# Stage ends by token tiles: tile 0's sums end first, and the next stage begins with two units in natural form

## The chip, the cores and the metric

The kernel runs on one core of one Trainium2 chip. The metric is the device time of one execution in microseconds; lower is better. Times are medians of a few runs on the chip, and the profile is one further execution. The engines are called PE (TensorE, the matrix engine), DVE (VectorE), ACT (ScalarE), POOL (GpSimd) and SP (SyncE, which here only issues DMAs).

## The reference

256 tokens of width 1024, float32, pass three layers. The first two (`first_block`) each mix tokens and then apply a feed-forward stage, with a layer norm after each; the second layer's feed-forward stage is a mixture of experts. The third (`second_block`) uses RMS norms ahead of its parts.

```python
for layer in range(2):
    mix = _mixer_ab(x, ...) if layer == 0 else _mixer_cd(x, ...)
    x = _layernorm(ALPHA * x + mix, ln_g[layer, 0], ln_b[layer, 0])
    ffn = _swiglu(x, w1_dense, w3_dense, w2_dense) if layer == 0 else _moe(x, w_router, w1_moe, w3_moe, w2_moe)
    x = _layernorm(ALPHA * x + ffn, ln_g[layer, 1], ln_b[layer, 1])
h = x
u = rms_norm(h, mix_norm_g)
proj = u @ w_in                       # q, k, v and the two halves of a gated convolution
h = h + concat(attention(q, k, v), conv(glu_a, glu_g)) @ w_out
u = rms_norm(h, ffn_norm_g)
h = h + (silu(u @ w_gate) * (u @ w_up)) @ w_down
return rms_norm(h, final_norm_g)
```

`_swiglu(x, w1, w3, w2)` is `(silu(x @ w1) * (x @ w3)) @ w2`, with a hidden width of 2816. `_mixer_cd` projects x to queries, keys and values of two attentions (c and d, 8 heads each) and to 8 forget columns, whose cumulated log-sigmoids are added to the scores of the first attention. The experts have a hidden width of 3584, and each token goes to 2 of 8.

## The kernel before

**Units and halves.** All weights come in units of 1 MB (128 partitions x 2048 floats) through a ring of 6 slots, loaded by SP in the order of their use. A product in full precision takes each operand as an upper part (rounded to PE's fp32r) and a lower part (the rest), and adds three products: upper x upper, upper x lower, lower x upper (`thirds`, L611 to L614). ACT writes the upper part of each unit (`upper`, L1270), DVE the lower (`lower`, L1697), into two buffers in turn; POOL makes the lower part of the first unit after the first mixer, after the dense FFN and after the third mixer (its `lower`, L2300). The experts use three buffers. `upper` waits until the unit before the last has been used, and PE waits for both parts of a unit (`taken`).

**Token tiles.** The tokens are two tiles of 128. A unit of columns is used in one of two forms. In the transposed form the weights are stationary and the 256 tokens move (`proj_transposed`, and `up`, L841 and L843, where upper and lower tokens move together in one matmul of 512 columns). In the natural form the tokens are stationary and 256 weight columns move (`proj_natural`). A unit of rows (`out_unit` for a mixer's output, `down` for an FFN's) adds to four PSUM banks of 512 columns: two tiles x two column halves.

**A stage end.** When the last unit has been added, DVE adds the residual (L1721), ACT forms the mean and the squared deviations (`deviations`, L1372 to L1374), POOL the reciprocal root (L2291), DVE centres (L1756) and scales (L1761) each tile; PE transposes the rows (L690), ACT copies their upper part (L1276), DVE their lower part (L1707); and the next stage's first unit begins. While PE has nothing to do it runs matmuls of ones whose results nobody uses (`keep_busy`, L605; `spins` says how many).

**The order of work** is written out by hand for each engine, and the engines meet by semaphores. In a mixer, the steps of the attention stand in numbered gaps, two per unit: lists such as `CD_SCORES` give for each step (scores, transposed probabilities, values) the gap in which it stands, and `CD_OUT_TURNED` the gaps in which finished heads are transposed for the output. `cd_gap(i)` exists on PE, ACT and DVE. The forget columns come from a narrow projection (`narrow`) at the start of the second mixer, and their lower parts from DVE (L2051).

## Time and profile before

| | us |
|---|---|
| median of 3 runs | 1795.64 (1794.57 to 1800.24) |
| the profiled execution | 1797.47 |
| its span, first to last instruction | 1795.6 |
| busy: PE | 1764.1 |
| busy: DVE | 1349.8 |
| busy: ACT | 1143.2 |
| busy: POOL | 156.9 |

The mean granted clock of TensorE was 0.997 of full speed. The span is what the page and the views of the trace divide up; the execution's own time is 1.9 us more. Matmuls are pipelined: a row's duration is longer than the distance to the next row, and the distance is the cost. The fillers count as busy.

### The profile page before, as it was taken

To read this page: it belongs to the slowest core of one execution; us is meant where nothing else is said; L and a number is where in the kernel's file an instruction comes from. 1 tells how busy PE (TensorE), PEld (TensorE's weight loads), DVE (VectorE), ACT (ScalarE), POOL (GpSimd) and SP (SyncE) were. 2 spreads that over 40 slices of the span, in tenths; PEclk is the share of its full clock that TensorE was granted. 3 is DMA by queue.
4 is the path that set the end of the run, shared out by engine and by line. 5 is a ranking of instruction groups with operands and counts; after the bars stand their busy time and mean duration, and the time that the engine had idled before them with its cause. 6 is when DMAs were issued, how large, how long until landed. Compare 5 with 4: busy or idle time off the path is not lost.

```text
span 1795.6 us, 24768 instructions
## 1 busy us (share of the span) xinstructions
PE 1764.1 (98%) x9332; PEld 1480.6 (82%) x9332; DVE 1349.8 (75%) x1252; ACT 1143.2 (64%) x1160; POOL 156.9 (9%) x107
## 2 busy tenths in 40 slices
PE   9999999999999999999999999999999999899998
PEld 7897888889878888888888888888888879878886
DVE  3765655545588888888888888888888888866555
ACT  4654545545467777777777777777777774545443
POOL 0002000100041000000000000000000105510000
PEclk9999999999999999999999999999999999999999
DMA  9845555543489999999999999999999985445550
GB/s 291 263 149 172 188 187 187 176 146 124 154 279 370 394 368 393 359 381 390 352 393 375 365 394 359 379 391 350 394 377 363 396 290 187 141 132 190 189 188 30
DMA packets 260196, 502.86 MB, mean 280 GB/s; under 512 B 15068, under 2 KB 101653, under 8 KB 259758
## 3 DMA queue, kind: packets, MB, share of 16 engines
q1 hardware_dynamic: 252160, 474.67, 74.6%
q0 software_dynamic: 7072, 26.69, 4.8%
q10 hardware_dynamic: 910, 0.76, 0.1%
q8 instruction: 36, 0.59, 0.1%
q14 instruction: 18, 0.15, 0.0%
HBM read 494.18 MB, written 12.65 MB: 282 GB/s over the span
## 4 chain that ended last, share of the span: by engine, by line
PE 90%; DVE 5%; ACT 2%; POOL 2%; issue 1%; DMA 0%; DVEq 0%; POOLq 0%; SPq 0%; ACTq 0%
PE psum L611 24%; PE psum L614 23%; PE psum L613 23%; PE psum L841 9%; PE psum L843 5%; DVE psum L2215 2%; PE psum L1126 1%; ACT wh L1270 1%; PE psum L750 1%; POOL wl L2300 1%; PE psum L718 1%; DVE x L1761 1%; POOL rstd L2291 1%; DMA ring<-in_w_in_ab 0%; PE psum L734 0%
## 5 line engine op out<-in xcount | busy, mean ns | idle before, releaser
L1697 DVE TENSOR_TENSOR wl<-ring,wh 128x2048 fp32r<-128x2048 f32 x437 | 1001.4, 2292 | 252.3 <-ACT wh L1270 251.2
L1270 ACT ACTIVATE wh<-ring 128x2048 fp32r<-128x2048 f32 x450 | 862.2, 1916 | 270.9 <-PE psum L611 169.6
L611 PE MATMUL psum<-wh,xT 128*128 128x512 f32 (+1 forms) x1136 | 431.6, 380 | 1.4 <-DVE xT L1853 1.1
L614 PE MATMUL psum<-wh,xT 128*128 128x512 f32 (+1 forms) x1136 | 424.5, 374 | 0.0
L613 PE MATMUL psum<-wl,xT 128*128 128x512 f32 (+1 forms) x1136 | 424.4, 374 | 0.0
L611 PE MATMUL psum<-wh,wnh 128*128 128x512 f32 x672 | 266.3, 396 | 0.5 <-DVE wnl L1853 0.5
L614 PE MATMUL psum<-wh,wnl 128*128 128x512 f32 x672 | 263.6, 392 | 0.0
L613 PE MATMUL psum<-wl,wnh 128*128 128x512 f32 x672 | 263.5, 392 | 0.0
L611 PEld LDWEIGHTS psum<-wh,xT 128*128 128x128 f32 x1136 | 214.2, 189 | 43.5 <-issue 3.0
L841 PE MATMUL psum<-xT,wh 128*128 128x512 f32 x704 | 249.1, 398 | 0.4 <-DVE xT L1707 0.4
L614 PEld LDWEIGHTS psum<-wh,xT 128*128 128x128 f32 x1136 | 214.0, 188 | 39.9
L613 PEld LDWEIGHTS psum<-wl,xT 128*128 128x128 f32 x1136 | 214.3, 189 | 37.0
L843 PE MATMUL psum<-xT,wl 128*128 128x256 f32 x704 | 197.4, 280 | 0.0
L841 PEld LDWEIGHTS psum<-xT,wh 128*128 128x128 f32 x704 | 132.2, 188 | 33.6 <-issue 1.2
L611 PEld LDWEIGHTS psum<-wh,wnh 128*128 128x128 f32 x672 | 126.3, 188 | 28.4 <-issue 1.4
L614 PEld LDWEIGHTS psum<-wh,wnl 128*128 128x128 f32 x672 | 126.2, 188 | 28.4
L613 PEld LDWEIGHTS psum<-wl,wnh 128*128 128x128 f32 x672 | 126.3, 188 | 25.8
L843 PEld LDWEIGHTS psum<-xT,wl 128*128 128x128 f32 x704 | 132.9, 189 | 0.7
L611 PE MATMUL psum<-xT,wh 128*128 128x256 f32 x384 | 112.4, 293 | 2.0 <-DVE wl L1697 1.7
L613 PE MATMUL psum<-xT,wh 128*128 128x256 f32 x384 | 109.9, 286 | 0.0
L614 PE MATMUL psum<-xT,wl 128*128 128x256 f32 x384 | 109.9, 286 | 0.0
L611 PEld LDWEIGHTS psum<-xT,wh 128*128 128x128 f32 x384 | 74.9, 195 | 4.4 <-issue 3.3
(303 smaller groups left out, 1410.9 us busy)
## 6 DMA issues: line engine op xcount, KB each, us to landing
ring<-in_w_moe SPq DMA_DIRECT2D x336, 1024.0 KB, 6.9
ring<-in_w_dense SPq DMA_DIRECT2D x33, 1024.0 KB, 5.2
ring<-in_w_in_ab SPq DMA_DIRECT2D x14, 1024.0 KB, 11.2
ring<-in_w_in_cd SPq DMA_DIRECT2D x12, 1024.0 KB, 5.3
ring<-in_w_gate SPq DMA_DIRECT2D x11, 1024.0 KB, 5.3
ring<-in_w_up SPq DMA_DIRECT2D x11, 1024.0 KB, 5.3
ring<-in_w_down SPq DMA_DIRECT2D x11, 1024.0 KB, 4.9
ring<-in_w_in SPq DMA_DIRECT2D x6, 1024.0 KB, 8.2
```

The source lines that it names most:

```text
L611: last = pe.matmul(o, a[0], b_[0], start=first, stop=False)
L613: pe.matmul(o, a[0], b_[1], start=False, stop=False)
L614: return pe.matmul(o, a[1], b_[0], start=False, stop=final)
L718: last = pe.matmul(o, q[rows, hp, t * P:(t + 1) * P], k[rows, hp, 0:n], start=True, stop=not (forget or masked))
L750: last = pe.matmul(to[:, o:o + HD], pT[:, g % 2, (2 * hh + s) * P:(2 * hh + s + 1) * P], v[:, s, h * HD:(h + 1) * HD], start=(s == 0), sto ...
L841: first_of(pe.matmul(ps.rearrange("p (a t) -> p a t", a=2), h_[:, k, m], xT_both[:, :, k, :], start=k == 0, stop=False))
L843: last = pe.matmul(ps[:, 0:T], l_[:, k, m], xTh[:, k, :], start=False, stop=k == KT - 1)
L1126: last = pe.transpose(bank[2 + c % 2][:, f * P:(f + 1) * P], mg[:, f * P:(f + 1) * P], ident[:, :])
L1270: act.activation(upper_half[i], ring[:, u_, :], ACT.Copy).then_inc(hi_ready[s_], 1)
L1697: dve.tensor_tensor(lower_half[i], ring[:, u_, :], upper_half[i].bitcast(F32), ALU.subtract)\
L1761: dve.scalar_tensor_tensor(x[:, t, s_], src[:, t, s_], rstd[:, t:t + 1], w[:, 1, s_], ALU.mult, ALU.add).then_inc(x_ready if t else x_half, 1)
L2215: last = dve.scalar_tensor_tensor(summed(c, j), upad[:, c, j:j + T], cw[:, c, j:j + 1], summed(c, j - 1), ALU.mult, ALU.add)
```

## The change

- The last two units of each mixer and of each FFN are added in another order (`out_last`, `down_last`): all of tile 0's sums end before the last three chunks of tile 1's.
- `tile_norms` takes the place of `layer_norm` after the first mixer, the dense FFN and the second mixer. Tile 0's mean and variance come from DVE (bn_stats, bn_aggr), tile 1's from row sums and ACT's squares as before (`second_deviations`). The RMS norm ahead of the last FFN is ordered likewise.
- After the first mixer, the dense FFN and the third mixer the next stage begins with `tile_pair`: two units in natural form, accumulated in banks 4 and 5 in four pieces (tile x half of the rows). With each piece PE adds both units' upper weight halves, and transposes the next piece in between; the products with the lower weight halves follow in a pass of their own, one unit after the other. For the FFNs the pair is the first unit of w1 and of w3, whose gated product is formed in natural form and transposed (`turn_hidden`); for the second mixer it is the two units of the first attention's values.
- DVE makes the lower parts that POOL made at the stage ends.
- These stages use a third buffer of halves, and `upper` waits there for one unit less (`used_before`).
- The steps of the first attention in the second mixer stand two gaps later, the next four steps one; the forget rows' lower parts stand ahead of one unit's lower half.
- The last unit of each FFN has its hidden parts in another order (`silus_last`, `gates_last`).

The core of the diff, its indentation shortened:

```diff
-CD_SCORES = [0, 1, 2, 3, 4, 5, 6, 7, 10, 11, 12, 13, 16, 17, 18, 19]
-CD_TURNED = [2, 3, 4, 5, 6, 7, 8, 9, 12, 13, 14, 15, 17, 18, 19, 20]
-CD_VALUES = [3, 4, 5, 6, 7, 8, 9, 10, 13, 14, 15, 16, 18, 19, 20, 21]
-CD_OUT_TURNED = [8, 14, 20, 22]
+CD_SCORES = [2, 3, 4, 5, 6, 7, 8, 9, 11, 12, 13, 14, 16, 17, 18, 19]
+CD_TURNED = [4, 5, 6, 7, 8, 9, 10, 11, 13, 14, 15, 16, 17, 18, 19, 20]
+CD_VALUES = [5, 6, 7, 8, 9, 10, 11, 12, 14, 15, 16, 17, 18, 19, 20, 21]
+CD_OUT_TURNED = [10, 14, 20, 22]
...
-CD_ORDER = [CD[n + h] + 256 * i for h in "cd" for i in range(2) for n in "qkv"]
+CD_ORDER = [CD["vc"], CD["vc"] + 256] + [CD[n + "c"] + 256 * i for i in range(2) for n in "qk"] + \
+   [CD[n + "d"] + 256 * i for i in range(2) for n in "qkv"]
...
+        after_out, after_ffn = (18, 53) if self.s == 0 else (11, 11 + 3 * NCH_D)
+        if self.s == 1 and n == 0:
+            half = 2
+        elif n >= LENGTHS[0]:
+            half = (LENGTHS[0] + 2 - n) % 3
+        elif after_out <= n < after_ffn:
+            half = (n - 16) % 3 if self.s == 0 else (after_out + 2 - n) % 3
         else:
-            half = (n + 1) % 2
+            half = n % 2
...
+    def used_before(self):
+
+        n = self.n - 1
+        third = n < 54 if self.s == 0 else True
+        back = 2 if n > (18 if self.s == 0 else 11) and third or n >= LENGTHS[0] else 1
+        return n - back + self.more
...
+    def tile_pair(src, n, done):
+
+        units = []
+        for j in range(2):
+            u_, loads, i, at_ = halves.place()
+            units.append([w.rearrange("p (k n) -> p k n", k=KT) for w in (upper_half[i], lower_half[i])]
+                         + [u_, loads, at_])
+        turn_piece(src, n, 0, 0)
+        keep_busy(5, 3)
+        for i, (t, kh) in enumerate(PIECES):
+            m = slice(t * P, (t + 1) * P)
+            pe.wait_ge(tr_low, trs[0] + i + 1)
+            for j, (h_, l_, u_, loads, at_) in enumerate(units):
+                o = bank[4 + j][:, t * 256:(t + 1) * 256]
+                if i == 0:
+                    pe.wait_ge(hi_ready[halves.s], at_ + 1)
+                for k in range(4 * kh, 4 * kh + 4):
+                    pe.matmul(o, xTh[:, k, m], h_[:, k, :], start=t == 0 and k == 0, stop=False)
+                    pe.matmul(o, xTl[:, k, m], h_[:, k, :], start=False, stop=False)
+                if j == 0 and i < 3:
+                    turn_piece(src, n, *PIECES[i + 1])
+        trs[0] += 4
+        for j, (h_, l_, u_, loads, at_) in enumerate(units):
+            pe.wait_ge(taken[halves.s][u_], loads)
+            for t in range(TT):
+                m = slice(t * P, (t + 1) * P)
+                for k in range(KT):
+                    last = pe.matmul(bank[4 + j][:, t * 256:(t + 1) * 256], xTh[:, k, m], l_[:, k, :],
+                                     start=False, stop=t == 1 and k == KT - 1)
+                    first_of(last)
+            last.then_inc(done[j], 1)
+            split_done()
...
+        two = split_unit("rows")
+        pe.wait_ge(o_low, turned)
+        sums_of(2, two, 0, (0, 1))
+        if gap is not None:
+            gap()
+        sums_of(2, two, 1, (0,))
+        three = split_unit("rows")
+        pe.wait_ge(o_low, turned + 1)
+        sums_of(3, three, 0, (0, 1))
+        sums_of(2, two, 1, (1,))
+        split_done()
+        sums_of(3, three, 1, (0, 1))
+        split_done()
+        sums[0] += 1
...
+        tile_pair(src, n, (one_done[s], up_done[s]))
         pe.wait_ge(sums_evac, sums[0])
-        up(s, 0)
-        up(s, 2)
-        down(s, 0, True, False)
+        up(s, 2, middle=turn_hidden)
+        down(s, 0, True)
...
+    assert steps[0] == STEPS_PAIR
+    tile_pair(x, 2, (step_done, step_done))
+    steps[0] += 2
+    for i in range(2):
+        projected["v", CD_FIRST // 4 + i] = STEPS_PAIR + 1 + i
+    pe.wait_ge(sums_evac, sums[0])
     narrow(later, 0, 8)
...
-    transposes(x, 3, spins=(16, 5, 2))
+    for j in range(2):
+        out_unit(j, 4 + j + 1, lambda: cd_gap(18 + 2 * j))
+        cd_gap(19 + 2 * j)
+    out_last(7, lambda: cd_gap(22))
+
+
+    transposes(x, 3, spins=(5, 7, 2))
...
+    def silu_pair(s):
+
+        act.wait_ge(one_done[s], 1)
+        act.activation(mh, bank[4][:, :], ACT.Silu).then_inc(silu_done[s], 1)
+        upper()
+        upper()
+        act.wait_ge(up_done[s], 2)
+        act.activation(hTh[:, 0, :, :], bank[6].rearrange("p (f t) -> p f t", f=2), ACT.Copy).then_inc(h_high[s], 1)
...
+    upper(a_pv, 8)
     upper()
-    deviations(0, y, u)
-    upper(sums_done, 1)
-    copy_transposed()
+    copy_piece(0, 0)
+    second_deviations(0)
+    for p in PIECES[1:]:
+        copy_piece(*p)
     ffn(0)
...
+    upper()
+    upper()
+    copy_piece(0, 0)
+    second_deviations(1)
+    for p in PIECES[1:]:
+        copy_piece(*p)
+    upper()
+    copy_step(nv[:, :, 0:256])
+    upper()
+    copy_step(nv[:, :, 256:512])
...
+    of_out = [(x2_ready, i + 1) for i in range(4)]
+    squares(of_out, (0,))
     upper()
-    squares([(x2_ready, i + 1) for i in range(4)])
-    upper(sums_done, 3)
-    copy_transposed()
+    copy_piece(0, 0)
+    squares(of_out, (1,))
+    for p in PIECES[1:]:
+        copy_piece(*p)
...
+        link(residual_half(0, 0, y, ALPHA, done, count))
+        dve.bn_stats(stat[:, 12:18], y[:, 0, 0:512])
+        residual_half(0, 1, y, ALPHA, done, count).then_inc(sums_ready, 1)
+        dve.wait_ge(sums_ready, 2 * n + 1)
+        link(dve.bn_stats(stat[:, 18:24], y[:, 0, 512:1024]))
+        link(dve.bn_aggr(mv[:, 0:2], stat[:, 12:24]))
+        first = ask_for(0, dve.tensor_scalar(e2[:, 0:1], mv[:, 1:2], LN_EPS, None, ALU.add))
+        norm_weights(n)
+        centred(0, mv[:, 0:1])
+        dve.wait_ge(rs_got, first)
+        normed(0, 0)
+        residual_half(1, 0, y, ALPHA, done, count, stat[:, 4:5])
+        residual_half(1, 1, y, ALPHA, done, count, stat[:, 5:6]).then_inc(sums_ready, 1)
+        dve.wait_ge(sums_ready, 2 * n + 2)
+        dve.nop().then_inc(sums_evac, 1)
+        if by_piece:
+            lower_piece(0, 0)
+        normed(0, 1)
+        dve.wait_ge(dev_ready, 2 * n + 1)
+        centred(1, stat[:, 6:7])
+        dve.wait_ge(dev_ready, 2 * n + 2)
+        second = ask_for(1, dve.tensor_scalar(e2[:, 1:2], ms[:, 1:2], 1.0 / D, LN_EPS, ALU.mult, ALU.add))
+        if by_piece:
+            lower_piece(0, 1)
+        dve.wait_ge(rs_got, second)
+        normed(1, 0)
+        normed(1, 1)
+        if by_piece:
+            lower_piece(1, 0)
+            lower_piece(1, 1)
...
+        if n_sq == 1:
+            summed(0, 0)
+            summed(0, 1)
+            mean_square(1, 0)
+            norm_weights(n)
+            dve.wait_ge(rs_got, squares_asked[2])
+            dve.wait_ge(x2_ready, 2)
+            scaled(0, 0)
+            summed(1, 0)
+            summed(1, 1)
+            dve.wait_ge(x2_ready, 4)
+            dve.nop().then_inc(sums_evac, 1)
+            lower_piece(0, 0)
+            scaled(0, 1)
+            mean_square(1, 1)
+            lower_piece(0, 1)
+            dve.wait_ge(rs_got, squares_asked[3])
+            scaled(1, 0)
+            scaled(1, 1)
+            lower_piece(1, 0)
+            lower_piece(1, 1)
+            return
...
+    def gate_pair(s):
+
+        lower()
+        dve.wait_ge(silu_done[s], 1)
+        dve.wait_ge(up_done[s], 1)
+        dve.tensor_tensor(mg, mh, bank[5][:, :], ALU.mult).then_inc(gated[s], 1)
+        lower()
+        dve.wait_ge(h_high[s], 1)
+        dve.tensor_tensor(hTl[:, 0, :, :], bank[6].rearrange("p (f t) -> p f t", f=2),
+                          hTh[:, 0, :, :].bitcast(F32), ALU.subtract).then_inc(h_low[s], 1)
...
+    tile_norms(sums_done, 1, True)
+    for _ in range(2):
+        lower()
     ffn(0)
-    layer_norm(y, down_done[0], NCH_D)
-
-
-    lower_transposed()
-    for _ in range(3):
+    tile_norms(down_done[0], NCH_D, True)
+
+
+    for _ in range(4):
...
+    lower()
+    for w in range(4, 12):
...
-    lower(0, 18)
...
-    lower(0, 18 + 3 * NCH_D)
...
-    lower(1, 11)
```

## Rows read from the trace of the kernel before

**Rows 1.** The page's busy times: us, share of the span, instructions.

```profile
PE 1764.1 (98%) x9332; PEld 1480.6 (82%) x9332; DVE 1349.8 (75%) x1252; ACT 1143.2 (64%) x1160; POOL 156.9 (9%) x107
```

**Rows 2.** Order of time, PE at stage end A: start us, us, operation.

```profile
160.97 3.81 PE L605 MATMUL psum<-spin 128*128 128x512 f32 x16
...
169.80 0.47 PE L841 MATMUL psum<-xT,wh 128*128 128x512 f32 x1 [0.26 <-DVE xT L1707]
```

**Rows 3.** Order of time, the other engines at stage end A.

```profile
158.44 0.69 DVE L1721 SCALAR_TENSOR_TENSOR y<-x,psum 128x512 f32<-128x512 f32 x1 [0.66 <-PE psum L614]
...
162.59 1.54 POOL L2291 TENSOR_TENSOR rstd<-small,half 128x1 f32<-128x1 f32 x1
...
164.25 0.75 DVE L1761 SCALAR_TENSOR_TENSOR x<-y,rstd,lnw 128x512 f32<-128x512 f32 x1 [0.54 <-POOL rstd L2291]
...
168.23 2.07 ACT L1276 ACTIVATE xT<-psum 128x512 fp32r<-128x512 f32 x4 [2.72 <-PE psum L690]
...
168.96 2.48 DVE L1707 TENSOR_TENSOR xT<-psum,xT 128x512 fp32r<-128x512 f32 x4 [0.60 <-ACT xT L1276]
...
181.17 0.39 ACT L1357 ACTIVATE tk<-psum 128x256 f32<-128x256 f32 x1 [1.03 <-PE psum L843]
```

**Rows 4.** Order of time, PE and ACT at stage end B.

```profile
354.30 3.81 PE L605 MATMUL psum<-spin 128*128 128x512 f32 x16
...
363.09 0.28 PE L611 MATMUL psum<-xT,wnh 128*8 128x256 f32 x1 [0.25 <-DVE xT L1707]
...
366.89 0.39 PE L611 MATMUL psum<-xT,wh 128*128 128x256 f32 x1
...
378.70 0.60 ACT L1286 ACTIVATE tk<-psum 128x512 f32<-128x512 f32 x1 [3.36 <-PE psum L614]
```

**Rows 5.** Order of time, PE and ACT at stage end D.

```profile
1595.26 2.91 PE L605 MATMUL psum<-spin 128*128 128x512 f32 x12
...
1613.83 0.39 ACT L1357 ACTIVATE tk<-psum 128x256 f32<-128x256 f32 x1 [2.45 <-PE psum L843]
```

**Rows 6.** DVE's groups by form: count, busy us and mean ns, idle before.

```profile
L1697 DVE TENSOR_TENSOR wl<-ring,wh 128x2048 fp32r<-128x2048 f32 x437 | 1001.4, 2292 | 252.3 <-ACT wh L1270 251.2
...
L2247 DVE BATCH_NORM_STATS2 small<-psum 128x6 f32<-128x512 f32 x2 | 1.4, 690 | 0.0
```

**Rows 7.** Order of time, the last out-transposition ahead of A.

```profile
152.32 0.60 PE L803 MATMUL psum<-ident,u 128*128 128x128 f32 x4
...
153.58 0.69 DVE L1853 TENSOR_TENSOR xT<-psum,xT 128x512 fp32r<-128x512 f32 x1 [0.27 <-ACT xT L1337]
```

**Rows 8.** Order of time, around the forget rows behind B.

```profile
386.99 2.29 DVE L1697 TENSOR_TENSOR wl<-ring,wh 128x2048 fp32r<-128x2048 f32 x1 [3.48 <-ACT wh L1270]
...
388.00 1.28 ACT L1304 ACT_TABLE_LOAD   x1
...
389.31 0.86 DVE L2051 TENSOR_TENSOR forget_r<-gnat,forget_r 8x256 fp32r<-8x256 f32 x2
...
390.27 0.46 PE L718 MATMUL psum<-tk,tq 64*128 64x128 f32 x3 [1.84 <-issue]
...
391.78 0.40 ACT L1304 ACTIVATE pr<-lg,small 128x128 f32<-128x128 f32 x1 [2.49 <-DVE small L1822]
```

**Rows 9.** Stretches: us, busy and instructions per engine, granted clock, DMA share, GB/s.

```profile
390.50:392.00 1.50, 1.50 (x12) 1.43 (x11) 0.84 (x2) 0.22 (x1) 0.00 (x0) 0.58 0.89 221
...
392.00:394.00 2.00, 2.00 (x11) 2.00 (x11) 0.00 (x0) 0.66 (x4) 0.00 (x0) 0.50 1.03 357
...
1568.00:1574.00 6.00, 4.82 (x36) 4.17 (x36) 1.53 (x4) 1.69 (x5) 0.42 (x1) 1.00 0.54 175
```

**Rows 10.** Order of time, PE and DVE in a heads gap behind B.

```profile
466.73 0.70 PE L718 MATMUL psum<-tb,ta 64*128 64x256 f32 x4
...
468.45 0.69 DVE L1822 TENSOR_REDUCE small<-lg 128x2 f32<-128x512 f32 x1
```

**Rows 11.** Order of time, DVE at stage end C.

```profile
497.82 1.42 DVE L1761 SCALAR_TENSOR_TENSOR x<-y,rstd,lnw 128x512 f32<-128x512 f32 x2
```

More of the change, by code:

```diff
@@ L845, in up, with down @@
                     split_done()
-            def down(s, c, first, final, shift=0):
+                    if w == 0 and middle is not None:
+                        middle()
+            def down(s, c, first, shift=0):
                 h_, l_ = split_unit("rows")
-                pe.wait_ge(h_low[s], 2 * c + 2 + shift)
-                for f, t, n in ([(f, t, n) for t in range(TT) for n in range(2) for f in range(2)] if final else
-                                [(f, t, n) for f in range(2) for t in range(TT) for n in range(2)]):
+                pe.wait_ge(h_low[s], 2 * c + 1 + shift)
+                for f, t, n in [(f, t, n) for f in range(2) for t in range(TT) for n in range(2)]:
                     m = slice(t * P, (t + 1) * P)
@@ L860, in down, with down_last, sums_of @@
                 split_done()
-            def ffn(s):
+            def down_last(s):
+                def sums_of(c, w, t, ns):
+                    m = slice(t * P, (t + 1) * P)
+                    for n in ns:
+                        n_ = slice(n * 512, (n + 1) * 512)
+                        for f in range(2):
+                            last = thirds(bank[4 + 2 * t + n][:, :], (w[0][:, f, n_], w[1][:, f, n_]),
+                                          (hTh[:, c % 2, f, m], hTl[:, c % 2, f, m]), False, c == 10 and f == 1, turned=True)
+                        if t + n == 2:
+                            last.then_inc(down_done[s], 1)
+                        elif c == 10:
+                            last.then_inc(sums_part, 1)
+                nine = split_unit("rows")
+                pe.wait_ge(h_low[s], 2 * 9 + 1)
+                sums_of(9, nine, 0, (0, 1))
+                sums_of(9, nine, 1, (0,))
+                ten = split_unit("rows")
+                pe.wait_ge(h_low[s], 2 * 10 + 1)
+                sums_of(10, ten, 0, (0, 1))
+                sums_of(9, nine, 1, (1,))
+                split_done()
+                sums_of(10, ten, 1, (0, 1))
+                split_done()
@@ new lines, in ffn, with turn_hidden @@
+            def ffn(s, src, n):
+                def turn_hidden():
+                    pe.wait_ge(gated[s], 1)
+                    for f in range(2):
+                        for t in range(TT):
+                            last = pe.transpose(bank[6][:, f * T + t * P:f * T + (t + 1) * P],
+                                                mg[:, t * 256 + f * P:t * 256 + (f + 1) * P], ident[:, :])
+                            first_of(last)
+                    last.then_inc(up_done[s], 1)
+                tile_pair(src, n, (one_done[s], up_done[s]))
@@ L1543, in _ @@
             cd_gap(22)
+            upper(a_pv, 24)
             upper()
[L1545 to L1546 removed]
+            second_deviations(2)
             copy_transposed()
@@ L1607, in _, with squares @@
             halves.at(1, 0)
-            def squares(waits):
-                for t in range(TT):
+            def squares(waits, ts=range(TT)):
+                for t in ts:
                     for h_ in range(2):
@@ L1723, in residual_half @@
                                                 accum_out=total[0] if total else None)
-            def residual(t, dst, alpha, done, n, totals):
-                for h_ in range(2):
-                    last = residual_half(t, h_, dst, alpha, done, n, stat[:, 4 * t + h_:4 * t + h_ + 1])
-                last.then_inc(sums_ready, 1)
-                dve.wait_ge(sums_ready, 2 * totals + t + 1)
-                if t == 1:
-                    dve.nop().then_inc(sums_evac, 1)
             def ask_for(t, ins):
@@ L1743, in layer_norm @@
                 asked = []
-                if sums:
-                    for t in range(TT):
-                        residual(t, src, ALPHA, *sums, totals=n)
                 norm_weights(n)
@@ L1775, in layer_norm, with tile_norms, centred, normed @@
                 normed(1, 1)
+                dve.wait_ge(x_ready, 2 * norms[0])
+                dve.wait_ge(x_half, 2 * norms[0])
+            def tile_norms(done, count, by_piece):
+                n = norms[0]
+                norms[0] += 1
+                w = lnw
+                def centred(t, mean):
+                    link(dve.scalar_tensor_tensor(x[:, t, :], y[:, t, :], mean, w[:, 0, :], ALU.subtract, ALU.mult))
+                def normed(t, h_):
+                    s_ = slice(h_ * 512, (h_ + 1) * 512)
+                    dve.scalar_tensor_tensor(x[:, t, s_], x[:, t, s_], rstd[:, t:t + 1], w[:, 1, s_],
+                                             ALU.mult, ALU.add).then_inc(x_ready if t else x_half, 1)
+                link(residual_half(0, 0, y, ALPHA, done, count))
[28 more added lines that the diff above has]
+                    lower_piece(1, 1)
                 dve.wait_ge(x_ready, 2 * norms[0])
@@ L2051, in _ @@
                 dve.tensor_tensor(forgets[r:r + 8, :], nfT, forgets[0:8, :].bitcast(F32), ALU.subtract).then_inc(forget_low, 1)
-            for w in range(3, 12):
+            lower()
+            for w in range(4, 12):
                 cd_gap(2 * w - 6)
@@ L2260, in _ @@
             lower()
-            halves.skip()
             rms_norm(u, 1, (x_half, x_ready), sums_done, 3)
-            lower_transposed()
-            lower()
+            for _ in range(2):
+                lower()
             ffn(1)
```

240 lines of the change are left out of this document (146 added, 94 removed).

## The prediction

> **What bounds the kernel now.** I read the page's busy times first: PE is busy 1764.1 of 1795.6 us [rows 1]. That leaves 31.5 us idle, but filler matmuls count as busy, so I read the four stage ends in order of time. I call them A (first mixer to dense FFN), B (dense FFN to second mixer), C (second mixer to router) and D (third mixer to last FFN), and count from E, the moment by which the last matmul of the ending sums has issued. At A fillers start at E = 160.97, and the first matmul of the next stage at 169.80: 8.8 us without work [rows 2]. The other engines' rows between show the chain that fills it: residual, row sums, rstd on POOL, normed halves, transposes, ACT's rounded copies, DVE's lower parts [rows 3]. The first two units of the next stage end at E+20.0: ACT's copy of the last product starts 181.17, 0.2 behind PE [rows 3]. At B the fillers start at E = 354.30 and the first two units have ended at 378.5, E+24.2, the narrow projection included [rows 4]; at D at E+18.4 [rows 5]. Between the stage ends PE goes back to back but for a few places that I come to, so a microsecond won or lost on PE at a stage end is one of the span.
>
> **Tile 0 earlier.** The last two units' work is reordered in chunks (six matmuls of 512 columns at 0.228, 1.37 us): 4 of them now follow tile 0's first half and 3 its second, where 3 and 2 did. So its residual halves start E-5.3 and E-3.9; the second one started E-2.5 (158.44) [rows 3]. Then bn_stats of the second half 0.7 [rows 6], bn_aggr, e2 and handovers 0.5, POOL's rstd 1.5 and the normed half 0.75 [rows 3]: the first normed half ends about E+0.5. Before it ended 165.00, E+4.0. What is late next is what follows.
>
> **The pair of units, A.** Behind that half DVE has tile 1's two residuals (0.7 each) and then a lower piece, so PE's first upper matmul is at E+2.8. Each later piece needs, in line, PE's eight matmuls for one unit (0.96, at 0.12 each: 96 took 11.6 from 366.89 to 378.5 [rows 4]), four transposes with the handover 0.6 [rows 7], ACT's copy 0.6 with its handover 0.1, DVE's subtraction 0.7 and 0.14 to PE [rows 3]: 3.1 us. PE has 2.3 us of work in it, so it idles 0.8 three times, and the fourth piece's lower part is done at E+12.1. Only then does DVE lower the pair's two weight units, of which POOL did one before: 2.29 each, E+14.4 and E+16.7 [rows 6]. The lower passes, 16 matmuls each, run E+14.5 to 16.4 and E+16.8 to 18.7.
>
> Up to here PE is 1.3 us ahead of before. But on ACT the next instruction after its last copy is the Silu of the first product, which waits for that unit's lower pass (E+16.4), and the upper half of the third unit stands behind it. Silu 0.6 ends E+17.2, the upper half takes 1.9 (E+19.1), DVE's lower half 2.3 (E+21.5), and PE begins the third unit at E+21.6. Before it began at E+20.0 without a wait. So PE idles 2.9 us, and A's resumption comes to +1.6. Added: a stall in the out stage, for unit 3 now has one chunk (1.4) between its transposes and its use; transposes begin 152.32, DVE's piece ends 154.27, 1.95 later, 0.3 of it under the transposes themselves: +0.3 [rows 7]. Four transposes of the hidden values, +0.4. ACT comes late to the fifth unit too, +0.2 (bounds 0 and 1). Sum +2.5.
>
> **Clock.** At 388.43 PE stood 1.84 us still [rows 8]; afterwards the granted clock was 0.58 for 1.5 us and 0.50 (1.2 GHz) for 2.0 us [rows 9], 1.6 us of clock lost; I take 1.5 of time. In a stretch with 4.82 busy of 6 us it stayed at 1.00 (2.4 GHz) [rows 9]. An idle of 2.9 lies beyond the first. I take a drop at A and at D, 1.5 each (bounds 0 and 3). A becomes +4.0.
>
> A table load could come on top at A, where ACT needs Silu's table. At 388.00 a load of 1.28 ran while its ACTIVATE waited on until 391.78 for DVE [rows 8], so I take this one as hidden under the wait, too. The Trainium skill (ScalarE: Activation LUTs, What ACT_TABLE_LOAD costs) has the load right before its ACTIVATE and prices a switch at about 2.66 us with its drain; by that, if all of it came after the wait, A would be 2.7 worse. The rows have it early and at 1.28, and the sum goes by them.
>
> **B.** The pair goes as at A, but ACT's next job after the copies is the third unit's upper half, and nothing waits for it. Pair to E+18.7, then narrow projection with evacuation and small transposes 3.8 (363.09 to 366.89 [rows 4]): the next projection begins E+22.6 against E+24.2, -1.6. The stall before 390.27: PE waited for the forget rows' lower part (389.31 to 390.17), which stood on DVE behind a full lower half (from 386.99, 2.29) [rows 8]. That lower half now comes after the rows, and ACT's copies before them ended about 388.0: -1.1, and with 0.7 us idle the clock has no reason to drop: -1.5. Against it, the second out-transposition is asked for in the same gap as the scores whose maximum it waits for: from the scores (466.73) to the end of the reduction (469.14) is 2.4, of which the gap's other work covers 1.8 [rows 10]: +0.6. The other heads move by one or two gaps with the same work, taken at 0 (bounds -1 and +2). B: -3.6.
>
> **C.** Only the norm and its place change. The last normed half ended 499.24, E+7.1 [rows 11]; now the second tile's chain (residuals to E+1.9, the first tile's half, centring to E+3.9, e2, rstd 1.0, two halves 1.4) ends E+6.8: -0.4, and the out stage's stall +0.3: -0.1. Fewer fillers leave an idle of 1.4.
>
> **D.** As A, with squares in place of row sums, and POOL no longer has a lower half ahead of rstd: first upper matmul E+2.5, third unit at E+21.3 against E+18.4, +2.9; hidden transposes 0.4, the fifth unit 0.2, clock 1.5; no stall in the out stage, whose transposes stand ahead as before. D: +5.0.
>
> **The rest.** Each FFN's last unit waits some 0.1 for its hidden lower part, since it starts a chunk sooner: +0.2. In the FFN loops a third buffer lets ACT run ahead of a PE that doesn't wait: 0. The DMAs are the same in number, in another order at B; slots come free up to 13 us later at A and D, four units ahead of use: 0 (bounds 0 and 1). POOL's DMAs of the norm weights move forward with it: 0.
>
> Sum: 4.0 - 3.6 - 0.1 + 5.0 + 0.2 = +5.5 us. The profiled execution took 1797.47 (span 1795.6), so 1803.0 in its terms; it lay 1.8 over the median of 1795.64, so the median comes to 1801.1.
>
> **Rivals.** (1) No drop of the clock in the two waits. For it: matmuls surround them; against it: 2.9 is over the 1.84 that did it. 3.0 less: 1798.1, no change that can be told. (2) The third unit isn't late at A and D, because the pieces pass faster than I have it and Silu with them. It decides at Silu's end: by E+14.3 PE never waits. Then 1.6 + 1.3 and 2.9 less and no drop: 5.5 - 5.8 - 3.0 = -3.3, 1792.3; with heads at B at their lower bound and the fifth unit on time about 1790.5. ACT's fixed order speaks against it, the kernel's 8.8 us gaps for it. (3) More of the same: the table load after its wait (+1.3 by the row), a drop also at C or inside the pair (+1.5), heads at B denser than they bear (+2): 1804 to 1806. For it: the thin fillers; against it: 4.82 busy of 6 at the full clock. (4) Tile 0's norm gains nothing, since something else holds the normed half (POOL, the norm weights): then A, B and D start some 3 us later each, 1810. POOL is free at A and B once its lower halves are gone; 0.03.
>
> **Numbers.** Forecast 0.38 (own range 1799 to 1803), rival 1 0.27, rival 2 0.17, rivals 3 and 4 0.18. About 5.4 us, 0.3%, is what a measurement can tell from none. Slower by that (over 1801.0) have rivals 3 and 4 and some 0.22 of the forecast: 0.40. Faster (under 1790.3): what I may have overlooked in favour, and most of rival 2, whose price is at that bound: 0.16. The rest, 0.44, is no change. The range is 1791 to 1806.
>
> **What would show it.** Right: PE idle close to 3 us before the first matmul of the third unit at A and D, released by DVE's lower half, with ACT's upper half just after a Silu; the granted clock at half behind it; the stall at the forget rows down from 1.84 to 0.7; B's next projection near E+22.6. Wrong: the pair ending well before E+18, or that upper half ahead of the Silu.

## The result, and the profile after

| | before | after |
|---|---|---|
| median of 20 runs each, same chip (us) | 1797.18 (1793.51 to 1800.49) | 1799.59 (1797.83 to 1802.74) |
| the profiled execution | 1797.47 | 1800.82 |
| its span | 1795.6 | 1799.0 |

The ratio is 1.0021, 95% interval 1.0014 to 1.0028: slower by 0.2%, less than the 0.3% taken as the bound of no change. The forecast was +5.5 us; the medians differ by 2.4, the profiled executions by 3.35.

The page's busy times of the changed kernel (us, share of the span, instructions):

```profile
PE 1756.4 (98%) x9348; PEld 1478.0 (82%) x9348; DVE 1357.0 (75%) x1246; ACT 1132.6 (63%) x1136; POOL 141.5 (8%) x104
```

PE is busy 7.7 us less than before [rows 1] and idle 42.6 us instead of 31.5: fillers went, and waits came. PE's list of waits says which (who waited, for whom, us in total, times, the longest):

```profile
PE psum L930 <- DVE wl L1880: 5.4, 2, 2.7
PE psum L757 <- DVE xT L1897: 4.9, 12, 0.5
...
PE psum L869 <- DVE small L2072: 1.2, 1, 1.2
PE psum L635 <- issue: 1.1, 1, 1.1
...
PE psum L784 <- issue: 0.5, 1, 0.5
```

The first line is the forecast's third unit, at A and D. The second is the pieces. The next two lines are waits in the second mixer's heads, and the last is the wait for the forget rows, which was 1.84 [rows 8].

PE in order of time at A, whose ending sums have issued at E = 160.58 (start us, us, operation, idle before and who ended it):

```profile
161.08 0.66 PE L736 MATMUL psum<-ident,x 128*128 128x128 f32 x4 [0.34 <-DVE x L1967]
161.49 1.41 PE L629 MATMUL psum<-spin 128*128 128x512 f32 x5
163.15 0.38 PE L757 MATMUL psum<-wh,xT 128*128 128x256 f32 x1 [0.25 <-DVE xT L1897]
...
166.20 0.39 PE L757 MATMUL psum<-wh,xT 128*128 128x256 f32 x1 [0.46 <-DVE xT L1897]
...
172.33 0.38 PE L757 MATMUL psum<-wh,xT 128*128 128x256 f32 x1 [0.46 <-DVE xT L1897]
...
174.53 4.37 PE L767 MATMUL psum<-wl,xT 128*128 128x256 f32 x32
181.61 0.58 PE L930 MATMUL psum<-xT,wh 128*128 128x512 f32 x1 [2.71 <-DVE wl L1880]
```

The useful work starts 2.6 us after E, where it started after 8.8 [rows 2]; but the third unit starts at E+21.03, where it started at E+20.0. ACT (first) and DVE in the same stretch show what holds it:

```profile
170.95 0.60 ACT L1414 ACTIVATE xT<-psum 128x512 fp32r<-128x512 f32 x1 [2.46 <-PE psum L736]
171.56 1.28 ACT L1520 ACT_TABLE_LOAD   x1
176.74 0.60 ACT L1520 ACTIVATE tk<-psum 128x512 f32<-128x512 f32 x1 [3.89 <-PE psum L767]
177.23 3.70 ACT L1395 ACTIVATE wh<-ring 128x2048 fp32r<-128x2048 f32 x2
```

```profile
160.27 0.75 DVE L1967 SCALAR_TENSOR_TENSOR x<-x,rstd,lnw 128x512 f32<-128x512 f32 x1 [0.53 <-POOL rstd L2569]
...
172.19 4.48 DVE L1880 TENSOR_TENSOR wl<-ring,wh 128x2048 fp32r<-128x2048 f32 x2
179.17 2.29 DVE L1880 TENSOR_TENSOR wl<-ring,wh 128x2048 fp32r<-128x2048 f32 x1 [2.50 <-ACT wh L1395]
```

ACT stands 3.89 us before the Silu, which waits for the first unit's low pass, with the third unit's upper half behind it. D is the same, with PE at 1615.35 and [2.71 <-DVE wl L1880]; its Silu:

```profile
1610.48 0.60 ACT L1520 ACTIVATE tk<-psum 128x512 f32<-128x512 f32 x1 [5.19 <-PE psum L767]
```

The clock, in stretches of 2 us (us, busy and count of PE, PEld, DVE, ACT, POOL, granted clock, DMA share, GB/s):

```profile
180.00:182.00 2.00, 0.39 (x2) 0.32 (x3) 2.00 (x3) 0.93 (x1) 0.00 (x0) 0.95 0.73 291
182.00:184.00 2.00, 2.00 (x8) 1.71 (x7) 2.00 (x2) 0.00 (x0) 0.00 (x0) 0.50 0.53 163
184.00:186.00 2.00, 2.00 (x10) 1.72 (x9) 0.26 (x1) 0.00 (x0) 0.00 (x0) 0.69 1.09 382
186.00:188.00 2.00, 2.00 (x14) 1.75 (x13) 0.00 (x0) 0.00 (x0) 0.00 (x0) 1.00 1.09 348
...
1616.00:1618.00 2.00, 2.00 (x9) 1.71 (x8) 2.00 (x1) 0.00 (x0) 0.00 (x0) 0.50 0.69 198
```

After each idle of 2.71 us the clock is at its lower level, 1.2 GHz, for over 3 us.

**Where the time went.** The span is cut at E of the four stage ends and at the first matmul of the experts (514.26 before, 513.29 after), and compared interval by interval, in us:

| interval | before | after | measured | forecast |
|---|---|---|---|---|
| start to A | 160.97 | 160.58 | -0.39 | +0.3 |
| A to B | 193.33 | 196.05 | +2.72 | +3.8 |
| B to C | 137.81 | 135.61 | -2.20 | -3.3 |
| C to the experts | 22.15 | 21.05 | -1.10 | -0.4 |
| experts to D | 1081.00 | 1081.55 | +0.55 | 0 |
| D to the end | 200.34 | 204.16 | +3.82 | +5.1 |
| sum | 1795.6 | 1799.0 | +3.4 | +5.5 |

The kernel before has its E's at 160.97 and 354.30 and 1595.26 [rows 2, 4, 5] and C's in this row:

```profile
492.11 2.23 PE L605 MATMUL psum<-spin 128*128 128x512 f32 x9
```

Of the changed kernel's, B's lies 0.50 ahead of its first row here, of which 0.34 is idle; C's and D's are the rows' starts, 492.24 and (0.01 less) 1594.84:

```profile
357.13 0.66 PE L736 MATMUL psum<-ident,x 128*128 128x128 f32 x4 [0.34 <-DVE x L1967]
...
492.24 1.31 PE L629 MATMUL psum<-spin 128*128 128x512 f32 x5
...
1594.85 0.60 PE L736 MATMUL psum<-ident,u 128*128 128x128 f32 x4
```

The +0.55 between the experts and D is no work of the change: it is 1.7 for a fall of the clock near 1475 that the kernel before didn't have in its profile (the last section), and -1.0 in the experts, where the code is the same (962.9 and 961.9 to the wait near 1475; 961.7 to 962.5 in the other runs). So an interval can be trusted to about 1 us where it holds the experts. From A to B and from D to the end it repeats to a tenth: the same code took 196.05, 196.09 and 196.12, and 204.16, 204.06 and 204.07 (the changed kernel and experiments 8 and 9). From the start to A it does not: the twelve profiles took 159.59 to 162.85 there, by how often the clock fell in it (last section), so the -0.39 is no effect of the change. Whole executions of one kernel lay up to 11 us apart.

### The profile page after: what moved, and what is told of

Its sections match the earlier page's. It is cut to its first block, busy times and chain, and to the rows that moved or that the text cites. A ratio compares the mean times of both kernels' runs of the same rounds, so it can differ in the third digit from the quotient of the medians.

```text
span 1799.0 us, 24772 instructions
## 1 busy us (share of the span) xinstructions
PE 1756.4 (98%) x9348; PEld 1478.0 (82%) x9348; DVE 1357.0 (75%) x1246; ACT 1132.6 (63%) x1136; POOL 141.5 (8%) x104
## 4 chain that ended last, share of the span: by engine, by line
PE 89%; DVE 6%; ACT 2%; issue 1%; POOL 1%; DMA 0%; DVEq 0%; POOLq 0%; SPq 0%; ACTq 0%
PE psum L635 23%; PE psum L637 23%; PE psum L638 23%; PE psum L930 8%; PE psum L932 4%; DVE psum L2494 2%; PE psum L1253 1%; ACT wh L1395 1%; PE psum L816 1%; DVE wl L1880 1%; PE psum L784 1%; PE psum L767 1%; PE psum L757 1%; PE psum L800 0%; POOL rstd L2569 0%
## 5 line engine op out<-in xcount | busy, mean ns | idle before, releaser
L1880 DVE TENSOR_TENSOR wl<-ring,wh 128x2048 fp32r<-128x2048 f32 x440 | 1007.5, 2290 | 191.5 <-ACT wh L1395 188.4
L635 PE MATMUL psum<-wh,xT 128*128 128x512 f32 (+1 forms) x1104 | 421.2, 382 | 1.6 <-DVE xT L2103 1.1
L638 PE MATMUL psum<-wh,xT 128*128 128x512 f32 (+1 forms) x1104 | 415.5, 376 | 0.0
L637 PE MATMUL psum<-wl,xT 128*128 128x512 f32 (+1 forms) x1104 | 415.4, 376 | 0.0
L635 PEld LDWEIGHTS psum<-wh,xT 128*128 128x128 f32 x1104 | 208.1, 188 | 43.7 <-issue 4.1
L638 PEld LDWEIGHTS psum<-wh,xT 128*128 128x128 f32 x1104 | 207.7, 188 | 38.9
L637 PEld LDWEIGHTS psum<-wl,xT 128*128 128x128 f32 x1104 | 208.1, 189 | 37.0
L930 PE MATMUL psum<-xT,wh 128*128 128x512 f32 x640 | 230.1, 401 | 5.4 <-DVE wl L1880 5.4
L932 PE MATMUL psum<-xT,wl 128*128 128x256 f32 x640 | 181.2, 283 | 0.0
L930 PEld LDWEIGHTS psum<-xT,wh 128*128 128x128 f32 x640 | 121.7, 190 | 35.5 <-issue 5.8
L932 PEld LDWEIGHTS psum<-xT,wl 128*128 128x128 f32 x640 | 121.9, 190 | 0.7
L638 PE MATMUL psum<-xT,wl 128*128 128x256 f32 x384 | 109.2, 284 | 0.0
L635 PEld LDWEIGHTS psum<-xT,wh 128*128 128x128 f32 x384 | 74.1, 193 | 4.3 <-issue 3.3
```

The source lines that it names most:

```text
L635: last = pe.matmul(o, a[0], b_[0], start=first, stop=False)
L637: pe.matmul(o, a[0], b_[1], start=False, stop=False)
L638: return pe.matmul(o, a[1], b_[0], start=False, stop=final)
L930: first_of(pe.matmul(ps.rearrange("p (a t) -> p a t", a=2), h_[:, k, m], xT_both[:, :, k, :], start=k == 0, stop=False))
L932: last = pe.matmul(ps[:, 0:T], l_[:, k, m], xTh[:, k, :], start=False, stop=k == KT - 1)
L1880: dve.tensor_tensor(lower_half[i], ring[:, u_, :], upper_half[i].bitcast(F32), ALU.subtract)\
```

## The experiments

Each was timed in five rounds against the kernel before, in three groups (1 to 4, 5 to 8, 9 and 10), each on another chip. The kernel before had medians of 1797.44, 1797.18 and 1799.91 us in them. That spread is as much as most of these edits are worth, so between groups the intervals say more than the medians. ACT's and DVE's order, and PE's, are written out by hand, so most edits move one call.

**1. ACT's upper half ahead of the Silu, at A and D.**

```
 def silu_pair(s):
+    upper()
     act.wait_ge(one_done[s], 1)
     act.activation(mh, bank[4][:, :], ACT.Silu)...
     upper()
-    upper()
```

> Against the changed kernel, ACT copies the third unit's upper half ahead of the Silu, at A and at D; nothing else differs. My theory: this order alone makes the third unit late. The copy then runs right behind the fourth piece's (some 171.6 to 173.5 at A), DVE's lower half follows the pair's two (176.7 to 179.0), and PE begins the third unit at E+18.4 instead of E+21.0, 0.6 after the pair: 2.1 us less idle at each of A and D, and without an idle of 2.7 the granted clock stays at 1.00, 1.6 less each. Sum -7.4: about 1792.2 beside 1799.6 of the changed kernel, 0.997 of the kernel before. Rival a, another wait takes its place (the gating product, which now stands behind that lower half, or the fourth unit's upper half behind the Silu): the first wait goes and one of 1 to 2 us comes back before the hidden transposes or the fourth unit; 1796 to 1799. Rival b, the clock falls from something else in the stage end (thin fillers, three idles in the pieces): the waits go, the clock's drop stays; -4.2, 1795.4.

Measured: 1791.47 us, ratio 0.9971 (0.996 to 0.9983). The third unit starts at E+18.45 at A (E = 161.07) and E+17.88 at D (E = 1589.74), with no wait ahead of it, and the clock behind it is 1.00:

```profile
179.52 0.47 PE L930 MATMUL psum<-xT,wh 128*128 128x512 f32 x1
```

```profile
180.00:182.00 2.00, 2.00 (x13) 1.74 (x13) 2.00 (x2) 0.00 (x0) 0.00 (x0) 1.00 1.02 400
```

A to B takes 191.90 (-4.15) and D to the end 199.86 (-4.30), each now shorter than before (193.33 and 200.34). No other wait took its place, which rules out rival a. One call's place on ACT, an engine busy 63% of the span, is worth 8 us. The table load stands in this run behind the upper half, and again ahead of the Silu's wait, at 173.88.

**2. The same at D alone.**

```
+    if s == 1: upper()
     act.wait_ge(one_done[s], 1)
     act.activation(mh, bank[4][:, :], ACT.Silu)...
+    if s == 0: upper()
     upper()
-    upper()
```

> As the run with the upper half first, but at D alone; A keeps the changed kernel's order. If the two places are worth the same (2.1 of wait and 1.6 of clock each): -3.7, 1795.9. If the price is mostly in the clock and that falls at A for another reason, D gives all of the whole experiment's gain.

Measured: 1795.68 us (0.9989, 0.998 to 0.9997). PE's list of waits keeps one of the two:

```profile
PE psum L930 <- DVE wl L1883: 2.7, 1, 2.7
```

A to B still takes 196.06, and D to the end 199.91. Half the gain with half the edit: the two places are worth the same.

**3. Fillers in the wait.**

```
 tile_pair(src, n, (one_done[s], up_done[s]))
 pe.wait_ge(sums_evac, sums[0])
+keep_busy(10, 3)
 up(s, 2, middle=turn_hidden)
```

> The changed kernel with ten filler matmuls (0.23 each) between the pair and the third unit at A and D: the wait stays, PE works through it. My theory: PE begins the third unit at the same time as in the changed kernel (E+21.0 at A, E+20.8 at D), but the granted clock stays at 1.00, so 1.6 less at each place: about 1796.4. Rival: the clock falls from what is ahead of it (PE idles three times in the pieces), and the fillers change nothing: 1799.6. A third: the idle of 2.7 costs no clock that counts, because what is slowed waits anyway for ACT and DVE: 1799.6 with the clock at 1.00.

Measured: 1796.70 us (0.9996, 0.9987 to 1.0006). PE at A, and the clock behind it:

```profile
181.02 2.44 PE L629 MATMUL psum<-spin 128*128 128x512 f32 x10
183.80 0.50 PE L930 MATMUL psum<-xT,wh 128*128 128x512 f32 x1 [0.34 <-DVE wl L1881]
```

```profile
184.00:186.00 2.00, 2.00 (x12) 1.72 (x12) 2.00 (x2) 0.00 (x0) 0.00 (x0) 1.00 0.40 71
```

The third unit starts at E+20.95, as late as ever, but from there to B's E takes 173.57 instead of 175.02, and from the third unit at D to the end 182.14 instead of 183.65. So the clock's fall costs 1.5 us at each place, and the wait is the rest. The forecast's separate 1.5 for the clock stands. The same two figures of the kernel before are 173.3 and 181.9 (E+20.0 and E+18.4): all that the hidden transposes, the fifth unit and the FFN's end cost together is 0.2, not 0.7.

**4. The kernel before, with the forget rows first.**

```
-lower()
 dve.wait_ge(step_evac, STEPS_FORGET)
 for r in (32, HD + 32): dve.tensor_tensor(forgets[r:r + 8, :], ...)
+lower()
```

> The kernel before with one edit: on DVE the lower half behind the forget rows' subtraction instead of ahead of it. My theory from the forecast: the stall of 1.84 us before the first scores shrinks to about 0.7, and the clock doesn't fall behind it: -1.1 -1.5 = -2.6, 1794.6 beside 1797.2. Rival: the lower half moved behind makes the next projection wait as long (it ends 2.3 later than the subtraction): no change, 1797.2. A second rival: only the stall's 1.1 goes, the clock's fall is worth nothing: 1796.1.

Measured: 1795.64 us beside 1797.44 (0.9992, 0.9983 to 1.0); by the intervals B to C falls from 137.81 to 135.01, -2.8. The first scores of the profile, against 390.27 with 1.84 [rows 8]:

```profile
388.72 0.46 PE L718 MATMUL psum<-tk,tq 64*128 64x128 f32 x3 [0.54 <-issue]
```

```profile
389.00:391.00 2.00, 2.00 (x21) 1.93 (x19) 2.00 (x2) 0.03 (x1) 0.00 (x0) 1.00 0.04 8
391.00:393.00 2.00, 2.00 (x20) 1.79 (x19) 0.82 (x3) 1.23 (x5) 0.00 (x0) 1.00 0.41 62
```

The stall shrinks by 1.3, and the clock doesn't fall, where it read 0.58 and 0.50 [rows 9]. One moved line carries more than half of what B gains (2.8 of 5.0, before what the heads cost there). The clock's share of it, some 1.5, rests on the one profile of the kernel before: behind the 0.54 or 0.55 that is left the clock didn't fall in any of eleven profiles, but whether it falls behind 1.84 each time is not shown. The median alone, 1.8 lower with an interval of the ratio that reaches 1, could not have told the rivals apart; the interval between two stage ends does.

**5. The order of the last two units undone.**

```
-sums_of(2, two, 1, (0,))
+sums_of(2, two, 1, (0, 1))
+split_done()
 three = split_unit("rows")
 sums_of(3, three, 0, (0, 1))
-sums_of(2, two, 1, (1,))
-split_done()
 sums_of(3, three, 1, (0, 1))
```

and likewise in `down_last`.

> The changed kernel, but the last two units of each ending sum are worked off one after the other, as before, so tile 0's sums end two chunks (2.7 us) later; the rest of the change stays. My theory from the forecast (tile 0 earlier carries the gain at each end): the first normed half ends E+3.1 instead of E+0.4, and everything up to the third unit shifts by that at A, B and D: +2.7 three times, +0.4 at C, -0.3 twice for the out stage's stall: about 1807.5 beside 1799.6. Rival a: the pieces are held by tile 1's norm and by the three idles anyway, so only some 1 us at each end comes back: 1803. Rival b: the order is worth nothing, because ACT's and DVE's chain to the third unit sets the resumption: 1799.6.

Measured: 1805.63 us (1.0042, 1.0025 to 1.0058), 6.0 over the changed kernel's median and between theory and rival a. PE at A, where E = 161.23:

```profile
163.08 0.66 PE L736 MATMUL psum<-ident,x 128*128 128x128 f32 x4 [1.70 <-DVE x L1965]
163.50 1.41 PE L629 MATMUL psum<-spin 128*128 128x512 f32 x5
165.16 0.38 PE L757 MATMUL psum<-wh,xT 128*128 128x256 f32 x1 [0.25 <-DVE xT L1895]
```

The first upper matmul is at E+3.93 instead of E+2.57 at A, the same at B, and E+2.77 instead of E+2.02 at D: 1.36 twice and 0.75. My expectation had miscounted. Before, two chunks followed tile 0's second half, and now three do: the order is worth one chunk, 1.37. The rest of the 3.5 us by which the first normed half comes sooner (E+0.44 instead of E+4.0) belongs to what this run keeps: the norm's own order, tile 0 through rstd and product before tile 1's sums are read, and at A a POOL without a lower half ahead of rstd. The two are not taken apart here. The intervals against the changed kernel: A to B +1.48, B to C +0.93, C to the experts (495.30 to 517.75) +1.40, D to the end +0.64. So at C, too, the order is worth one chunk, where I had expected 0.4; that tile 1's chain waits on DVE behind tile 0's would explain it, and is not tested. The four intervals make 4.45; no place that was edited shows the rest of the median's 6.0.

**6. Halves between the pieces.** ACT copies the third unit's upper half, and DVE lowers the pair's first unit, while they stand idle ahead of the fourth piece.

```
 copy_piece(1, 0)
+upper()
 copy_piece(1, 1)
 ...
 lower_piece(1, 0)
+lower()
 lower_piece(1, 1)
```

with one `upper()` and one `lower()` less behind, and `CD_OUT_TURNED = [10, 15, 20, 22]` as in experiment 8.

> The changed kernel with three moves. At A, B and D ACT copies the third unit's upper half between the third and the fourth piece (it stands idle 2.5 us there, the copy takes 1.9), DVE lowers the pair's first unit in the same place (idle 2.4, the half takes 2.3), and the second mixer's second out-transposition is asked for one gap later (as in the run with that alone). My theory: the pair then ends when PE is through with it, E+17.8, and the third unit follows without a wait: against the upper half first alone (E+18.4, 1791.5), -0.6 at A and D, -0.5 at B, -1 for the out-transposition: about 1789. Rival: DVE's half between the pieces is some tenths late each time and pushes the fourth piece, so what is won behind it is lost ahead of it: 1790.5 to 1791.5.

Measured: 1789.52 us (0.9961, 0.9949 to 0.9973). The third unit starts at E+17.63 at A and E+17.05 at D, 0.8 sooner than in experiment 1, and A to B takes 191.10 (-0.8). The copy of 1.9 and the subtraction of 2.3 fit their gaps of 2.5 and 2.4 and delayed no piece.

**7. The pieces turned early.**

```
+if j == 0 and i == 2:
+    turn_piece(src, n, *PIECES[3])
 for k in range(4 * kh, 4 * kh + 4):
+    if j == 0 and i == 1 and k == 4 * kh + 2:
+        turn_piece(src, n, *PIECES[2])
     pe.matmul(...)
     ...
-if j == 0 and i < 3:
+if j == 0 and i == 0:
     turn_piece(src, n, *PIECES[i + 1])
```

with ACT's order and the list of experiment 6, and DVE's of the changed kernel.

> As the run between the pieces, but DVE lowers no half there, and PE turns the third piece after a quarter of the second piece's matmuls and the fourth ahead of all of the third's, so that the copy and subtraction run under PE's work. My theory: the pieces' idle of 0.46 goes at the fourth and part of it at the third, the fourth piece is lowered near E+11, but then DVE's three halves in a row (6.7) set the third unit: E+17.8, as between the pieces; about 1789, no better than that run. Rival: the pieces' period was what counted, and PE gains 1.2 at each of three ends: 1786 to 1787. Second rival: PE waits for tile 1's normed halves with the transposes ahead of its matmuls, and loses: 1792 or more.

Measured: 1786.98 us (0.9951, 0.9938 to 0.9965). The idle of 0.46 ahead of the third and fourth pieces is gone, and the third unit starts at E+17.36 at A and E+16.80 at D, 0.25 sooner than in experiment 6: DVE's three halves in a row do set it, as I had it. A to B, B to C and D to the end are 0.20, 0.53 and 0.29 shorter, 1.0 together, where I had expected nothing and the rival 1.2 at each of three ends. The median, 2.5 below experiment 6's, lies where the rival had it (1786 to 1787); the intervals bear out 1.0 of that. The profile of experiment 6 had the clock's fall at the third mixer's wait and this one's hadn't, so the rest may be chance.

**8. The second out-transposition a gap later.**

```
-CD_OUT_TURNED = [10, 14, 20, 22]
+CD_OUT_TURNED = [10, 15, 20, 22]
```

> The changed kernel with the second mixer's second out-transposition asked for in gap 15 instead of 14, one gap behind the scores whose maximum it waits for. PE stood 1.2 us there, where I had put 0.6. My theory: the wait goes, -1.2, 1798.4. Rival: the rotation only moves on to the unit's own copy and subtraction, which are now one gap closer to their use: 1799.6 or some tenths more.

Measured: 1798.58 us (1.0002, 0.999 to 1.0014). B to C takes 134.36, 1.25 less, and the wait of 1.2 is gone from the list without a new one. It had been forecast at 0.6.

**9. The third group of heads in bank 5.**

```
-group_values(..., bank[(4, 5, 4, 3)[s // 4]], 1 + s // 4)
+group_values(..., bank[(4, 5, 5, 3)[s // 4]], 1 + s // 4)
...
-pe.wait_ge(a_done, 5)
...
+if late and i == 2:
+    pe.wait_ge(a_done, 5)
```

with the same bank in DVE's `group_normed`, and the chunks of the first output unit (`late`) in the order kk, n, t, so that the first two don't need that bank.

> The changed kernel; in the second mixer the third group of heads sums its values in bank 5 instead of 4, and the first output unit begins with the chunks of banks 4 and 6, so that it waits for that group's normed values only before its third chunk (1.37 us later). In the changed kernel PE stands 1.07 us before that unit, which it did not before. My theory: moving the heads' gaps one later put the group's last values right ahead of the unit whose sums take over their bank; with the bank free the 1.07 goes: 1798.5 beside 1799.6. Rival: what holds PE is something else at that place (the unit's lower half, or its transposed input), and the wait stays: 1799.6.

Measured: 1798.73 us (0.9999, 0.9984 to 1.0013). B to C takes 134.31, 1.30 less. The wait in the changed kernel, what DVE does just ahead of it, and PE in the same place here:

```profile
463.55 0.47 PE L635 MATMUL psum<-wh,wnh 128*128 128x512 f32 x1 [1.07 <-issue]
```

```profile
462.76 0.69 DVE L2079 TENSOR_TENSOR u<-psum,small 128x512 f32<-128x512 f32 x1
```

```profile
463.53 1.00 PE L816 MATMUL psum<-nw,pT 128*128 128x64 f32 x8
464.34 0.48 PE L635 MATMUL psum<-wh,wnh 128*128 128x512 f32 x1
```

"issue" means that the profile shows no releaser. It was the explicit wait for the third group's normed values, which end 0.10 ahead of PE (at 463.45) and which the new lists put one gap later, right ahead of the unit that takes over their bank. The forecast had these heads "with the same work, taken at 0".

**10. All of it.** Experiment 7 with the edits of 9.

> The pieces turned early, the third unit's upper half between the pieces, the second out-transposition a gap later, and the third group of heads in bank 5 with its late wait. My theory: the gains add, since each is PE idle at a place of its own: 1787.0 - 1.1 = 1785.9, 0.9937 of the kernel before. Rival: what is gained in the heads is lost again at the second mixer's end, where DVE comes with tile 0's sums: 1787.

Measured: 1785.67 us beside 1799.91, ratio 0.9921 (0.99 to 0.9942). That is 0.8% under the kernel before in this group, where that kernel was 2.5 to 2.7 us slower than in the others; beside their 1797.18 and 1797.44 it is 0.65%. It is 13.9 us under the changed kernel's median, though the two were not timed side by side. B to C takes 131.92, 1.32 less than experiment 7's 133.24, while A to B (190.81 and 190.90) and D to the end (198.78 and 198.79) are the same; PE's list has neither of the heads' two waits. What is left at the top is outside the stage ends:

```profile
PE psum L847 <- ACT pr L1462: 3.6, 4, 1.2
PE psum L1285 <- DVE nv L2472: 2.4, 1, 2.4
PE psum L761 <- DVE xT L1907: 2.2, 6, 0.5
```

The gains added up. The rival, by which they would be lost again at C, didn't come true.

## Why the prediction was right, and where its sizes were off

The sign, the place and the mechanism held. The third unit waits at A and at D, behind ACT's Silu, and the clock falls behind each wait. Undoing just that order takes away 8 us (experiments 1 and 2), so rival 2, in which the unit isn't late, is what the change would have been with one call moved. Rival 1, no fall of the clock, is out by the stretches, and rival 4 by the normed half at E+0.4. The total was forecast 2.1 too high against the profiled span and 3.1 too high against the medians. The median alone would not have told the forecast from rival 1, whose +2.5 is nearer to the measured +2.4 than the forecast's +5.5; the idles of 2.71 and the stretches behind them do. The range of 1791 to 1806 held rivals 1 and 2 as well, so that the time lay in it says little; the rows say that the path was right. By term:

- **Third unit.** Forecast E+21.6 and E+21.3, measured E+21.03 and E+20.51. The wait was forecast 2.9 and is 2.71; the chain of pieces is 3.06 a piece, as forecast (3.1), with 0.46 of PE's idle in each where 0.8 was forecast, and starts at 2.57 (2.02 at D, where the transposes follow E without a wait). Net cost +1.0 and +2.1 instead of +1.6 and +2.9.
- **Clock.** Forecast 1.5 twice, measured 1.5 twice (experiment 3).
- **Hidden transposes, fifth unit, the FFNs' last unit.** Forecast 0.7 at each end, measured 0.2. The fifth unit wasn't late.
- **The out stage's stall.** Forecast +0.3 at A and at C. PE's rows have no such wait: in the 20 us ahead of E none reaches 0.1, at A or at C.
- **B, the resumption.** Forecast E+22.6, measured E+22.0 (the first projection starts at 378.60, and E is 356.63), so -2.2 instead of -1.6.
- **B, the forget rows.** Forecast -2.6, measured -2.8 alone (experiment 4; its clock's share rests on one profile), and the stall is 0.55 in the changed kernel.
- **B, the heads.** This is the step that failed. The forecast had +0.6 for the out-transposition and 0 for the other heads; they cost 1.25 and 1.3 (experiments 8 and 9). The first was priced by what the gap's other work covers, read in another gap [rows 10]; gap 14 covered 1.45 us instead of 1.8. The second was argued away: equal work, moved by one gap, does not end equally far ahead of the unit that reuses its bank. -2.2, -2.8, +1.25 and +1.3 make -2.45, where -2.20 was measured; 0.25 is open. The bounds of -1 and +2 for the other heads held the 1.3.
- **C.** Forecast -0.4, measured -1.10: the last normed half ends at 498.28, E+6.0 and not E+6.8.
- **The table load.** It ran at 171.56, just behind the fourth piece's copy and under the wait of 3.89, at 1.28 us. The Trainium skill (ScalarE: Activation LUTs, What ACT_TABLE_LOAD costs) prices a switch of table at some 2.66 us with its drain; here 0.01 us passed between the copy's end and the load, and the Silu followed its releaser, so nothing of it was on the path. At D, where Silu's table was in place, ACT stood still for 5.19 us ahead of the Silu, which is A's 3.89 and the load, and the wait for the third unit is 2.71 as well.

The errors in A, C and D all made the change look worse than it was, and the heads at B better, so the total came nearer than its parts. That is luck.

## What to carry to other kernels

When the work at a seam is cut finer, so that PE can start sooner, ask of each engine that feeds it, and that works off its list in order as ACT does here, which instruction stands behind the new wait: here a weight copy that needed nothing stood behind a Silu that needed the new, shorter chain's end, and it cost more than the finer cut had won (4.15 against 1.4 us from A to B). Put what is ready ahead of what waits, and into the idle gaps that the cut itself makes. When gaps are renumbered, check each bank's last reader against its next writer; "the same work" has a new neighbour. And time such a change by intervals between fixed events of the profile as well as by the median, which here moved as much from chance as from most of the edits.

## What the runs showed of the hardware

An idle of one length made the clock fall in one execution and not in the next. Every kernel here has the same wait of 2.38 us (2.37 before) ahead of the same eight matmuls of the third mixer. In 7 of the 12 profiles the granted clock fell right behind it, in 5 it stayed at 1.00. Ahead is the changed kernel's, then experiment 1's:

```profile
1475.18 5.39 PE L1279 MATMUL psum<-y,nv 128*128 128x512 f32 x8 [2.38 <-DVE nv L2462]
```

```profile
1471.65 3.70 PE L1279 MATMUL psum<-y,nv 128*128 128x512 f32 x8 [2.38 <-DVE nv L2462]
```

The same matmuls took 1.69 longer. Behind the idles of 2.71 it fell nine times of nine (at A and D in the changed kernel and in experiments 5, 8 and 9, at A in experiment 2), and behind the 1.84 of the kernel before in the one profile that there is; it did not fall behind 0.54 in experiment 4, nor in the pieces with 0.46 three times, nor at C with 0.9 and 0.5.

Shorter idles can do it too, so their length alone doesn't decide. The first mixer has a wait near 125 us that took 1.32 to 1.34 in all twelve profiles, and behind it the clock fell in 7 of them. Experiment 9's, then experiment 6's (the wait in order of time, then stretches):

```profile
125.09 0.49 PE L784 MATMUL psum<-tk,tq 64*128 64x128 f32 x4 [1.34 <-DVE wnl L2105]
...
126.00:128.00 2.00, 2.00 (x16) 2.00 (x15) 1.97 (x3) 0.60 (x1) 0.00 (x0) 0.77 0.00 0
128.00:130.00 2.00, 2.00 (x12) 2.00 (x11) 0.02 (x1) 0.88 (x4) 0.00 (x0) 0.50 0.71 188
```

```profile
125.13 0.49 PE L784 MATMUL psum<-tk,tq 64*128 64x128 f32 x4 [1.34 <-DVE wnl L2109]
...
128.00:130.00 2.00, 2.00 (x19) 2.00 (x17) 0.07 (x1) 0.88 (x4) 0.00 (x0) 1.00 0.68 168
```

Behind a wait of 1.68 to 1.70 near 73 us it fell in none of the twelve. In three (the kernel before, the changed one, experiment 9) it fell near 35 us, with no idle longer than 0.34 in the 20 us ahead, and in two (experiments 3 and 6) near 15 us, behind 1.46 and 1.44.

Each fall costs 1.5 to 1.7 us. The interval from the start to A shows it a second time: it took 159.59 and 159.67 in the two profiles without a fall there, 160.58 to 161.23 in the eight with one, 162.56 and 162.85 in the two with two. That chance is a part of why executions of one kernel lie some us apart, and why a median of a few moves by as much as most of these edits.
